# The first feed-forward with seven block products for eight in three of its four groups, and its conditioning sums spread over later stages

## What is computed

```python
c_act = jax.nn.silu(c)
for i in range(DEPTH):                      # DEPTH = 2
    mod = c_act @ ada_w[i] + ada_b[i]       # conditioning: 1024 x 6144 per layer
    sh1, sc1, g1, sh2, sc2, g2 = jnp.split(mod[:, None, :], 6, axis=-1)
    h = rmsnorm(x, norm_g[i, 0]) * (1.0 + sc1) + sh1
    y = mlstm_mixer(...) if i == 0 else sgu_mixer(...)
    x = x + g1 * rmsnorm(y, norm_g[i, 1])
    h = rmsnorm(x, norm_g[i, 2]) * (1.0 + sc2) + sh2
    y = jnp.square(jax.nn.relu(h @ ffn_w1[i])) @ ffn_w2[i]     # 1024 -> 4096 -> 1024
    x = x + g2 * rmsnorm(y, norm_g[i, 3])
```

## Time and profile before

| | |
|---|---|
| median of the runs | 2058.39 us |
| profiled execution | 2058.68 us, span 2056.9 us |
| PE busy | 2019.9 us, 98% |
| DVE busy | 1223.0 us, 59% |
| ACT busy | 882.6 us, 43% |
| POOL busy | 114.4 us, 6% |
| loads of `ada_w` from ACT's queue | 40 of 1 MB, 5.2 us to landing |
| loads of `ffn_w` | 64 of 1 MB from SP's queue, 3 accumulating from POOL's |
| mean granted clock | 0.996 |

### The profile page before, as it was taken

The page is one execution under the profiler, slowest core; times in us unless marked ns, Lnnn a source line. Parts: engine busy times, 40 slices in busy tenths (PEclk is TensorE's granted clock), DMA queues, the critical chain, the costliest instruction groups (busy, mean ns, idle before and its releaser), DMA issues.

```text
span 2056.9 us, 27536 instructions
## 1 busy us (share of the span) xinstructions
PE 2019.9 (98%) x10822; PEld 1686.5 (82%) x10822; DVE 1223.0 (59%) x1805; ACT 882.6 (43%) x1300; POOL 114.4 (6%) x103
## 2 busy tenths in 40 slices
PE   6999999999999999999999999999999999999998
PEld 4898888888887888988888888876777798888887
DVE  4668857666566345655674735345579736545455
ACT  3333473424247222346454446245455545324233
POOL 0000010000001015100000001000211000000000
PEclk9999999999999999999999999999999999999999
DMA  9562337666553523333434332310132133323321
GB/s 317 164 237 92 116 109 234 196 220 202 184 174 102 164 82 103 96 73 109 161 81 127 123 98 92 121 62 11 57 105 86 42 113 103 103 82 103 103 72 72
DMA packets 225821, 251.52 MB, mean 122 GB/s; under 512 B 11026, under 2 KB 211117, under 8 KB 224805
## 3 DMA queue, kind: packets, MB, share of 16 engines
q1 hardware_dynamic: 181824, 202.45, 31.1%
q10 hardware_dynamic: 42293, 44.27, 6.6%
q0 software_dynamic: 1584, 3.15, 0.9%
HBM read 240.77 MB, written 8.42 MB: 121 GB/s over the span
## 4 chain that ended last, share of the span: by engine, by line
PE 93%; DVE 3%; DMA 1%; ACT 1%; issue 1%; DVEq 1%; SPq 0%; ACTq 0%; POOL 0%; POOLq 0%
PE bank L728 31%; PE bank L800 26%; PE bank L1282 6%; PE bank L1264 5%; PE bank L902 4%; PE bank L1414 4%; PE bank L831 2%; PE bank L972 2%; PE bank L1386 1%; PE bank L1397 1%; PE bank L1116 1%; PE bank L1361 1%; PE bank L1470 1%; PE bank L1455 1%; PE bank L1364 1%; PE bank L1237 1%
## 5 line engine op out<-in xcount | busy, mean ns | idle before, releaser
L728 PE MATMUL bank<-h_hi,w_both_hi 128*128 128x512 f32 x464 | 182.4, 393 | 0.0
L728 PE MATMUL bank<-h_lo,w_both_hi 128*128 128x512 f32 x464 | 181.2, 391 | 0.0
L728 PE MATMUL bank<-h_hi,w_both_lo 128*128 128x512 f32 x464 | 181.1, 390 | 0.0
L2259 DVE TENSOR_TENSOR w_both_lo<-raw,w_both_hi 128x2048 fp32r<-128x2048 f32 x52 | 119.1, 2290 | 68.0 <-ACT w_both_hi L1540 68.0
L2259 DVE TENSOR_TENSOR u_both_lo<-raw,u_both_hi 128x2048 fp32r<-128x2048 f32 x50 | 114.2, 2290 | 76.2 <-ACT u_both_hi L1540 76.2
L1540 ACT ACTIVATE u_both_hi<-raw 128x2048 fp32r<-128x2048 f32 x50 | 94.8, 1907 | 122.4 <-PE bank L800 77.4
L728 PE MATMUL bank<-h_hi,u_both_hi 128*128 128x512 f32 x368 | 143.5, 390 | 0.0
L728 PE MATMUL bank<-h_hi,u_both_lo 128*128 128x512 f32 x368 | 143.2, 389 | 0.0
L728 PE MATMUL bank<-h_lo,u_both_hi 128*128 128x512 f32 x368 | 143.2, 389 | 0.0
L1540 ACT ACTIVATE w_both_hi<-raw 128x2048 fp32r<-128x2048 f32 x50 | 94.8, 1907 | 95.8 <-PE bank L800 44.1
L800 PE MATMUL bank<-u_both_hi,g_hi 128*128 128x512 f32 x312 | 123.5, 396 | 0.0
(11 more groups left out here) (504 smaller groups left out, 5089.8 us busy)
## 6 DMA issues: line engine op xcount, KB each, us to landing
raw<-in_ffn_w SPq DMA_DIRECT2D x64, 1024.0 KB, 5.3
ada_raw<-in_ada_w ACTq DMA_DIRECT2D x40, 1024.0 KB, 5.2
raw<-in_w_up SPq DMA_DIRECT2D x22, 1024.0 KB, 5.1
raw<-in_b_w_in SPq DMA_DIRECT2D x16, 1024.0 KB, 5.4
raw<-in_w_in SPq DMA_DIRECT2D x15, 1024.0 KB, 5.5
raw<-in_a_w_in SPq DMA_DIRECT2D x12, 1024.0 KB, 6.2
ada_head<-in_ada_w SPq DMA_DIRECT2D x8, 1024.0 KB, 12.2
raw<-in_b_w_out SPq DMA_DIRECT2D x8, 1024.0 KB, 7.2
```

The costliest lines, as they stand in the source:

```text
L728: mm = pe.matmul(o, x, y, start=(k == 0 and j == 0), stop=(k == kc - 1 and j == 2))
L2259: dve.tensor_tensor(lo, raw[s][:], f32(hi), ALU.subtract).then_inc(sem("split_done"), 1)
```

## The change

`ffn0` now runs the same code as `ffn1` (`ffn(st, ...)` with `st` 0 or 1): three fast groups, and the fourth as usual. With that come these moves.

- The conditioning sums of `ffn0` are made in 28 halves: 512 rows by 512 columns, four instructions of 128x512 (`ada_half_sum`). Six stand in the three fast groups, nine in the fourth group, five in `b_in`, four in `b_out` and four in `ffn1`. The seven rounds of `ada_rows4`, copy and `ada_turn4` stand once in the fast groups of `ffn0` (r = 0), twice in its fourth group, twice in `b_in`, once in `b_out` and once in `ffn1`.
- Their loads go into one buffer `ada_half`, or in the fourth group of `ffn0` into two in turn (`ada_half_x`). A load into a buffer is issued when the sum out of it is done: by POOL for most, by SP for the odd ones of the fourth group, by ACT for the four in `b_out`.
- The block sums live in `X` now, so `x` is written to memory at the start of each feed-forward and read back near its end, 2 MB each way. In `b_in` SP loads `lnb_bc` when the sums of that stage are done, and `ws_raw` after round 4 is turned.
- The fifth product has banks 6 and 7 in place of 4 and 5, and the loops over groups are written out.

The core of the diff, with the lines that set the order of the sums:

```diff
-            def ada_rows4(n, a):
-                pe.wait_ge(sem("ada_summed"), a + 4)
+            def ada_rows4(r):
+                pe.wait_ge(sem("ada_summed"), 24 + 4 * r)
...
+            def ffn(st, name, came_from):                       # PE
+                first_pair(came_from, t0, q0)
+                for g in range(FAST):
+                    for j in range(0 if g else 2, 4):
+                        fast_up(st, g, j)
+                        if st == 0 and (g, j) == (2, 2):
+                            ada_rows4(0)
+                        if st == 0 and (g, j) == (2, 3):
+                            ada_turn4(0)
...
+                    for m in range(7):
+                        fast_product(st, g, m)
...
@@ b_in, PE
                     tok_pair(t0 + 2 * i, q0 + i, "WU"[i % 2], h_hi, h_lo)
+                if i == 1:
+                    ada_rows4(3)
+                if i == 2:
+                    ada_turn4(3)
+                    ada_rows4(4)
+                if i == 3:
+                    pe.wait_ge(sem("gy_col"), 3)
+                    ada_turn4(4)
...
@@ b_in, ACT
                     if i:
                         for c in (2 * s, 2 * s + 1):
                             v_gelu(i, c)
+                if i >= 2:
+                    ada_row_copy(i + 1)
...
@@ b_out, ACT
                 split(u0 + i // 2, i % 2, 4 * (q0 + i // 2), "UWU"[i // 2])
+                if i < 3:
+                    ada_in_out(21 + i)
...
+            def ada_half_sum(n):                                # DVE
+                unit, half = n // 2, n % 2
+                o = acc_ring[unit % 3]
...
+                for k in range(4):
+                    which = c_act[:, 4 * half + k:4 * half + k + 1]
+                    if half == k == 0:
+                        i = dve.tensor_scalar(o, w[:, k], which, None, ALU.mult)
+                    else:
+                        dve.drain()
+                        i = dve.scalar_tensor_tensor(o, w[:, k], which, o, ALU.mult, ALU.add)
+                i.then_inc(sem("ada_summed"), 1)
...
+                for j in range(6):                              # ffn0, fourth group, DVE
+                    rest(u0 + 1 + j // 2, s, "UW"[j // 2 % 2])
+                    if st == 0:
+                        if j < 5:
+                            ada_half_sum(6 + 2 * j)
...
+                    if st == 0 and j < 4:
+                        ada_half_sum(7 + 2 * j)
...
+            def ada_load(n):                                    # POOL
+                pool.wait_ge(sem("ada_summed"), 20 + n - (1 if 7 <= n < 15 else 0))
+                pool.dma_start(ada_buffer(n)[:], ada_cols(n)).then_inc(sem("ada_late"), 16)
...
+            def ada_in_out(n):                                  # ACT
+                act.wait_ge(sem("ada_summed"), 20 + n)
+                act.dma_start(ada_buffer(n)[:], ada_cols(n)).then_inc(sem("ada_in"), 16)
```

More of the change, by code:

```diff
@@ L59 @@
 NCOL = at
-PHASES = [("a_in", 12, 2), ("a_out", 4, 2), ("ffn0", 32, 2), ("b_in", 16, 2), ("b_out", 8, 2), ("ffn1", 10, 2),
+PHASES = [("a_in", 12, 2), ("a_out", 4, 2), ("ffn0", 10, 2), ("b_in", 16, 2), ("b_out", 8, 2), ("ffn1", 10, 2),
           ("in2", 8, 2), ("low", 4, 7), ("gates", 8, 2), ("out2", 4, 2), ("conv", 34, 2)]
@@ L509, in t5_rows, with fast_in @@
                 sp.dma_start(t5_dram[:, rows], bandm[:].unsqueeze(1).broadcast_to([WH, 8, 512])).then_inc(sem("t5_out"), 16)
[L511 to L531, removed]
+            def fast_in(st, g, name, src):
+                which = FAST_IN[FAST * st + g, name][0]
+                sp.dma_start(f_raw[fast_raw(g, name)][:].rearrange("p (k n) -> p k n", n=src.shape[2]), src).then_inc(sem(which), 16)
@@ L565, in _ @@
                     tile_in(j % 2, r3(j % 2), cols(w2[:, g, :], j * 256, 256), T0["b_out"] + 4 * g + j)
-                gy_write(2 + g)
+                if g == 0:
+                    gy_write(2)
             sp.wait_ge(sem("sgu_y"), NSGU)
             gy_read(2)
[L569 to L576, removed]
@@ L1285, in _ @@
-            for g in range(FAST):
-                for j in range(0 if g else 2, 4):
-                    fast_up(g, j)
-                for m in range(7):
-                    fast_product(g, m)
-            for j in range(4):
-                tile(t0 + 2 + j, j % 2, q0 + 1 + j // 2, h_hi, h_lo, parts=slot("WU"[j // 2], j % 2),
-                     added=fast_added(FAST - 1, 6, 0) if j == 0 else None)
-            tok_pair(t0 + 6, q0 + 3, "W", g_hi, g_lo, ready=(sem("ffn_g"), G0["ffn1"] + 4))
@@ L1294, in _ @@
-            last_pair("ffn1", t0 + 8, q0 + 4, "U", g_hi, g_lo)
+            ffn(1, "ffn1", "b_out")
             t0, q0 = T0["in2"], N0["in2"] // 4
@@ new lines, in fast_s1, with fast_sum @@
+            def fast_s1(st, g, ks):
+                dve.wait_ge(sem("f_g"), 24 * st + 8 * g + 4 + ks.stop)
+                dve.tensor_tensor(s_sum[:, ks], quarter(1, 0)[:, ks], quarter(1, 1)[:, ks], ALU.subtract).then_inc(sem("f_sum"), 1)
+            def fast_sum(st, g, to, more):
+                which, n = FAST_IN[FAST * st + g, more]
+                dve.wait_ge(sem(which), n)
+                a, b = (f_raw[fast_raw(g, name)][:] for name in (to, more))
+                dve.drain()
+                dve.tensor_tensor(a, a, b, ALU.add).then_inc(sem("f_sum"), 1)
@@ L2879, in _ @@
-            for j in range(6):
-                s, q = j % 2, q0 + 1 + j // 2
-                rest(u0 + 1 + j // 2, s, "UW"[j // 2 % 2])
-                for b in range(2):
-                    if j < 4:
-                        m, y = 2 * s + b, 2 * j + b
-                        dve.wait_ge(sem("ffn_ghi"), GHI0["ffn1"] + y + 1)
-                        dve.tensor_tensor(g_lo[:, y], T[m][:], f32(g_hi[:, y]), ALU.subtract).then_inc(sem("ffn_g"), 1)
-                    else:
-                        y_part(q, 2 * s + b, 0, True)
```

873 lines of the change are left out of this document (453 added, 420 removed).

## The result

The changed kernel took 2068.48 us (median of five, 2066.38 to 2070.44) beside 2058.6 for the kernel before: a ratio of 1.0047 with a 95% interval of 1.0033 to 1.0062. It is slower, by about 10 us. The forecast was 2057.1, with 2048 to 2064 as the range, so the time lies outside it, on the side that I had given 0.22. The profiled execution, 2066.38 us with a span of 2064.6, is the fastest of the five.

What follows compares the result with a forecast made beforehand. TensorE, busy 98% of the span, was taken as the bound. 2058.68 − 16.3 + 4.1 + 1.9 + 5.8 + 3.2 = 2057.4, or 2057.1 in terms of the runs; range 2048 to 2064 for 8 in 10.

Steps and rivals of the forecast that it cites:

- the side that I had given 0.22: Whole kernel: a time slower than 2062.5 us, mostly from slow POOL loads or `ffn0`'s fast groups losing pace; chance 0.22.
- The saving of 16.3 us: Three groups of `ffn0`: 72 fewer matmuls at 0.2266 us each, -16.3 us, fast groups running without a wait of PE.
- The half's price: Conditioning sums on DVE: a half of four dependent 128x512 instructions takes 3.25 us, ends 2.7 and 4.4.
- `b_in`, third pair: End of that pair: PE's `ada_rows4(4)` waits for half 19, started after the last bias: +4.1 us, plus 1.6 of clock.
- fourth pair: End of that pair in `b_in`: `ada_turn4(4)` waits for ACT's row copy behind the last gelu, +1.9 us.
- L: Issue to landing of a plain 1 MB load from POOL's queue: 5.9 us taken, with 5.2 and 8.6 as ends.
- the slower rival: POOL's plain loads take 8.6 us like the accumulating ones, delaying `b_in` and `ffn0`'s fourth group: 2064 us, chance 0.2.
- `b_out`: Start of that stage: half 21 ahead of the second tile's `rest` delays the second pair, +5.8 us, plus 1.6 of clock.
- The fourth group: Last group of `ffn0`, nine halves and two turns: no wait of PE without a late load, 0 us.
- the other moves: `x` written out and read back, small loads, bank swap: zero, with up to 2 us against it.
- The clock: Behind the longer waits in `b_in` and `b_out`: a half-clock stretch costing 1.6 us each, +3.2 us in all.
- The second rival: Slow POOL loads of 8.6 us: half 12 in `ffn0`'s fourth group at about 1221, a wait of 2.8 us; chance 0.2.

Runs made afterwards that it cites:

- bin: Changed kernel with only `b_in` reordered: `ada_turn4(3)` and `ada_rows4(4)` inside the fourth pair, ACT's row copies ahead of the last two gelus: 2058.51 us, ratio 1.0002.
- gy2: Changed kernel with the `gy_rows` write of `b_out` moved behind SP's eighth load: 2060.90 us, ratio 1.0022 to the kernel before.
- packed: Changed kernel with all four `gy_rows` writes in place but as 128 pieces of 32 bytes, gate's row in another order: 2054.92 us, ratio 0.9997.
- beforepacked: Kernel before the change with its `gy_rows` writes as 128 pieces of 32 bytes, gate's row in another order: 2057.78 us, ratio 0.9999.
- gy1: Changed kernel with the `gy_rows` write of `ffn0` moved behind the reload of `x`: 2064.46 us, ratio 1.0042 to the kernel before.

## Why the prediction was wrong

**The saving of 16.3 us** was right, with its argument that the fast form runs at the bare distance: 81.60 us a group, and a kernel without the waits is 17 to 18 us below before.

**The half's price** of 3.25 us was right: four dependent 128x512 took 3.23 together, and the first half of a unit 0.49 + 2.40 with the gap between, 2.95 for my flat 3.25.

**`b_in`, third pair**, 5.7 forecast and 6.0 measured, and **fourth pair**, 1.9 and 2.0: right, and bin shows the cause to be the two orders named. Part of the first wait is one that I had put at nothing: `ada_turn4(3)` waits 1.72 us for ACT's copy before half 19's 1.77. The end is that of half 19, as worked out.

**L, the time of a plain load of POOL's**: 5.9 taken, 5.6 the median. So the slower rival, which rested on 8.6 for every such load, was wrong in its mechanism, though the side was right.

**`b_out`**, 7.4 forecast and 13.1 measured. The step that failed is "ACT issues the load of half 21 when half 20 is summed, so it lands at 849.6 + 5.2". The order was right, as gy2 shows with 7.3, and the load's time was not: I took the median of ACT's loads for a load beside `gy_rows`, and it took 10.5. That is 5.7 of the miss.

**The fourth group**, 0 forecast and 7.1 measured. The step that failed is "without a late load". I had followed half 12, in `ffn1`'s times, and not half 6, whose load POOL can issue only when half 5 is summed, 1.9 us before DVE wants it. With 5.6 us that is a wait of DVE alone; with 15 it reaches PE. And I had noted of the other moves that "The small loads and the bank swap have no reader that is near" and put them at zero. The write of `gy_rows` isn't even named there; it has no near reader, but the loads beside it had. That is 7.1 of the miss.

Together 12.8 us, for a miss of 2068.5 − 2057.1 = 11.4. What is common to both is one cause, which packed and beforepacked show: 1024 pieces of 4 bytes. The trace of before held a sign of it that I had not looked for. From 840 to 860 us, with the write issued at 842.00, the loads of `b_out`'s weights took 11.6 us at the median, where those of all of `b_in` took 5.4. TensorE didn't wait for them, and beforepacked, where they are fast, shows the write to be the cause:

```profile
raw<-in_b_w_out SPq DMA_DIRECT2D x3, 1024.0 KB, 11.6
```

**The clock** was forecast at 1.6 us behind each of two longer waits. By the same figure, with only what stands behind a wait, it was 1.8, 2.2 and 2.3 us behind the three of the changed kernel, and 1.4 to 2.7 over all runs. Behind the wait of 1.8 us at the fourth pair it was nothing in three of the four traces that have it, but 1.6 in gy1's. The pause from which I read the price also ended sooner than I said: matmuls of 128x512 run from 248.80 on, not from 249.2. And none of the nine other traces has such a stretch at that place, with the same small matmuls, so a pause of this kind doesn't always bring one.

The rest of the sum comes out as written. The second rival's 2.8 us for the fourth group doesn't follow from its own numbers: half 12 at 1221 is 1.8 us behind the 1219.23 at which TensorE asks, and 2.5 with the one `g_lo` of 0.69 that stands between.

The Trainium skill, "DMA: Bandwidth & Descriptors", section "Rules for kernel authors", says that a last dimension that isn't contiguous becomes one descriptor per element and should be rearranged; the trace agrees, with 13.8 us for 4 KB in this form and 5.3 when packed. The same page's section "Queues, rings and completion order" says that each DMA engine takes turns between the queues for which it has work, packet by packet. Taking turns alone doesn't account for what the trace shows: the load on POOL's queue, q0, was issued at 527.40, and from 528 to 534 us only SP's queue, q1, moved anything, 0.39 MB. What the runs do show is that another issuing queue was no shelter: loads of SP, POOL and ACT were all late beside this write.

```profile
q1 hardware_dynamic: 427, 0.39, 121.0%
```

What stays open is what exactly is held up inside the DMA. In `ffn0` the engines read as fully busy while little moved:

```profile
528.00:538.00 10.00, 10.00 (x46) 8.26 (x44) 1.30 (x1) 3.73 (x6) 0.15 (x1) 1.00 1.12 109
```

A share of 1.12 at 109 GB/s stands against 0.94 at 295 in the stretch from 550.80. In `b_out` they were nearly idle instead. From 840 to 842 us nearly all of the small packets went (first line), and from 842 to 849 hardly anything moved (second line), 0.11 MB of it on ACT's queue for the load of 844.04. The rest of that load came after 849, when the write, landing 12.6 us after 836.75, was done:

```profile
DMA packets 1327, 0.28 MB, mean 141 GB/s; under 512 B 1056, under 2 KB 1327, under 8 KB 1327
DMA packets 57, 0.13 MB, mean 19 GB/s; under 512 B 0, under 2 KB 0, under 8 KB 56
```

In `ffn0` 1056 packets of under 512 B likewise went from 527 to 529 us, and the write landed at 537.2. So in both places the small packets were through in about 2 us and the loads were held for longer than that. Engines full of small packets are not the picture; what it is that waits, and why the engines read busy in one place and idle in the other, no run here tells.

## What to carry to other kernels

Before a load is given a near use, look what else is in flight at its issue: a transfer of a few KB that takes over 10 us to land is a warning, even where nobody waits for it, and the median time of a load does not hold beside it. A sum put behind the last evacuation of a block, with TensorE's next step waiting for it, costs its full length plus the clock that TensorE loses; put inside the next block it costs nothing. When an edit makes no difference to the time, compare the places before dropping the theory: gy1 had removed 7 us and made 5 elsewhere.

## What the runs showed of the hardware

- A write of 4 KB as 1024 pieces of 4 bytes took 11.2 to 15.3 us to land in `ffn0` and `b_out` of the changed kernel and its variants (10.2 to 15.3 over all four writes), and as 128 pieces of 32 bytes 3.8 to 5.3 there (3.6 to 9.7 over all). Loads of 1 MB issued within some 12 us behind it, from three different queues, took 10.5 to 15.6 us in `ffn0` of the changed kernel and in `b_out` of both; the same ones with the packed write took 5.2 to 8.7.
- Each wait of TensorE between 2.8 and 11 us behind the start of `ffn0` had a clock of 0.50 behind it, for 3.3 to 6.1 us, worth 1.7 to 2.7 us. One of 1.8 us had it in one trace of four, and one of 2.3 us, at 1490 us in the kernel before, had none.
- Dependent 128x512 multiply-adds of DVE took 0.75 us each and stood 0.83 apart: a chain of four took 3.23.
- 1 MB loaded from POOL's queue landed in 5.6 us (median of 20), beside 5.1 for `ada_half` from ACT's and 5.4 for `ffn_w` from SP's; the accumulating form had taken 8.6.
